# The first block's 88 projection tiles in seven products of quarters

## The chip, the cores and the metric

The kernel runs on one core of one Trainium2 chip. The metric is device time in microseconds (us); lower is better. PE is TensorE (its matmuls; PEld its weight loads), DVE VectorE, ACT ScalarE, POOL GpSimd, SP SyncE, which issues the weight transfers.

## The reference

A token sequence of 16 meta tokens and 256 real ones (width 2048, float32) goes through two blocks. The first block is one layer:

```python
xn = rmsnorm(h, norm_g[l])
(a_q, a_f, a_i, a_z, b_q, b_k, b_v, b_o, b_ig, b_fg, b_z,
 c_r, c_k, c_v, c_wd, c_ad, c_z, g_a, g_b, g_c) = split_cols(xn @ w_in[l])
y_a = hgrn2_mixer(a_q, a_f, a_i, a_z, ...)      # branch A
y_b = mlstm_mixer(b_q, b_k, b_v, b_o, b_ig, b_fg, b_z, ...)   # branch B
y_c = rwkv7_mixer(c_r, c_k, c_v, c_wd, c_ad, c_z, ...)   # branch C
merged = sigmoid(g_a) * (y_a @ w_br[l, 0]) + sigmoid(g_b) * (y_b @ w_br[l, 1]) + sigmoid(g_c) * (y_c @ w_br[l, 2])
h = h + merged @ w_out[l]
```

The mixers use silu and sigmoid of several of these projections (silu(q), sigmoid(f), sigmoid(-f), silu(z) in A; silu after a short convolution, sigmoid(o), silu(z) in B; two sigmoids of low-rank products and silu(z) in C). The second block has two layers of another kind (pooling, state space, sparse attention), each with a large input projection of its own. The product that this change touches is `xn @ w_in`, with 2048 terms for each output.

## The kernel before

Activations lie with features on the 128 partitions and the 272 tokens along the free axis (`xnT`: 16 pieces of 128 features). A tile is 128 output columns of a projection for all tokens: 16 matmuls, each with a 128x128 piece of weights held and 272 columns of `xnT` (256 where meta tokens aren't needed) streamed, summed in a PSUM bank. `ring` has four slots of 2 MB of weights, 256 columns (two tiles) each; SP fills them in order, each when the tiles of its last use are done. `section_pe` (line 289) does eight tiles from the four slots; tiles alternate between banks 0 and 1, and `section_act` (line 339) copies each into a field of `G` (`g[0]` to `g[6]`), a field being eight tiles.

The first block runs in this order on PE: eight raw tiles of branch A's q (line 307), during which the inputs are normalised; A's other 24 tiles; A's mixer with the gate tiles g_a (line 481, into `hT`) between its small products; the merge with w_br (line 515); B's 24 tiles, the input and forget gates (line 853), 8 tiles of z; B's mixer; merge; in C a low-rank tile (line 1117), 8 tiles of k, the low-rank products up (line 1127), 8 of r, the norms (line 544), 8 of v, the dot products (line 1139), 8 of z, then C's mixer. 88 tiles of these go through `section_pe`. Sigmoids are computed as exp on ACT, plus one and reciprocal on DVE (`plus_one_inverse`, lines 562 and 564), over a whole field at a time.

The second block's large projection is already done in *units* (line 367): weights and inputs are cut in quarters, and two tiles come out of seven products instead of eight. A product is eight matmuls of 128 or, with the meta tokens, 144 columns. A unit needs turned inputs (four sums and differences of quarters of `xnT`: x12, x22, x21, x11, made once) and four sums of quarters of its own weights, which DVE makes in the ring's last slot (s1, s2, s4, lines 419, 422, 432) or in place (line 428), so that three slots are left for loads. PE's seven products go to two banks, `own` and `other`; some of their intermediate states are copied out by ACT (`unit_first_act`, `unit_middle_act`, `unit_last_act`) and added by DVE (`unit_ends_dve`). The counters are `st_full` (PE), `st_act`, `st_dve` and `st_sum`; `proj_full` and `proj_free` count tiles, `work_full` and `work_free` the uses of four further banks (2 to 5, taken in turn, `wbank`), which the mixers use for small products. The order on every engine is that of the code; every wait is on a counter, and behind a waiting instruction everything on its engine waits.

## Time and profile before

| | |
|---|---|
| median of 3 runs | 3409.15 us (3408.1 to 3411.21) |
| profiled execution, its own time | 3415.68 us |
| its span | 3413.9 us |
| PE busy | 3379.4 us, 22582 instructions |
| PEld busy | 2949.7 us |
| DVE, ACT busy | 1577.5 us, 639.8 us |
| mean granted clock | 0.994 |

The profile is of one execution. Busy time of PE runs over pipelined matmuls whose ends are modelled, so stretches and starts tell more than durations. A line is that of the kernel's source; a matmul in float32 leaves two records and two weight loads. In the chain of waits each piece is a stretch in which the named line held up everything after it.

### The profile page before, as it was taken

The page shows a single profiled execution, that of the slowest core. Times are in us where ns is not written, and L with a number is a line of the kernel's source. Part 1 is how long each engine was busy: PE and PEld are TensorE (multiplying, and loading weights), DVE is VectorE, ACT ScalarE, POOL GpSimd, SP SyncE. Part 2 cuts the span into 40 slices and gives each one's busy share as a digit, 9 for nine tenths or more (in the row PEclk, how much of TensorE's full clock was granted, in tenths as well). Part 3 has the DMA queues.
Part 4 walks back from the last instruction along what each step waited for, and adds up shares of the span by engine and source line. Part 5 has one row for each costly group of instructions (what it writes and reads, how often), then busy time and mean ns, then how long its engine had stood idle before and what let it go on. Part 6 is the DMA issues. An engine that isn't in the chain of part 4 may idle for free.

```text
span 3413.9 us, 53363 instructions
## 1 busy us (share of the span) xinstructions
PE 3379.4 (99%) x22582; PEld 2949.7 (86%) x22582; DVE 1577.5 (46%) x2834; ACT 639.8 (19%) x1632; POOL 45.0 (1%) x83
## 2 busy tenths in 40 slices
PE   9999999999999999999999999999999999999999
PEld 7888888888888898888899997877779999988787
DVE  2426631324556471522455756524344566563343
ACT  1012200011011000111111216412131112352211
POOL 1000000000000000000000000000000000000000
PEclk9999999999999999999999999999999999999999
DMA  7443244433444302553444444333444544533432
GB/s 233 136 152 114 100 148 147 149 124 112 154 128 144 99 4 70 203 170 104 141 156 149 157 149 139 87 124 118 142 128 148 166 148 157 173 124 87 145 127 74
DMA packets 436422, 454.89 MB, mean 133 GB/s; under 512 B 25307, under 2 KB 412832, under 8 KB 435904
## 3 DMA queue, kind: packets, MB, share of 16 engines
q1 hardware_dynamic: 433600, 444.48, 41.1%
q0 software_dynamic: 2128, 5.19, 0.5%
q8 instruction: 175, 2.87, 0.4%
q10 hardware_dynamic: 464, 1.90, 0.1%
q14 instruction: 55, 0.45, 0.0%
HBM read 449.46 MB, written 2.10 MB: 132 GB/s over the span
## 4 chain that ended last, share of the span: by engine, by line
PE 98%; DVE 1%; ACT 0%; DVEq 0%; issue 0%; POOL 0%; ACTq 0%; POOLq 0%
PE bank L367 21%; PE bank L289 19%; PE bank L2063 10%; PE bank L481 10%; PE bank L1952 9%; PE bank L307 5%; PE bank L515 5%; PE bank L2127 3%; PE bank L1602 3%; PE bank L1162 3%; PE bank L2036 1%; PE bank L2114 1%; PE bank L2086 1%; PE bank L544 0%; PE bank L1989 0%; PE bank L687 0%
## 5 line engine op out<-in xcount | busy, mean ns | idle before, releaser
L289 PE MATMUL bank<-xnT,ring 128*128 128x272 f32 (+1 forms) x2816 | 633.2, 388 | 1.6 <-ACT wk L912 1.0
L289 PEld LDWEIGHTS bank<-xnT,ring 128*128 128x128 f32 x2816 | 535.2, 190 | 99.2 <-issue 3.3
L481 PE MATMUL bank<-xnT,ring 128*128 128x256 f32 x1536 | 343.7, 383 | 0.7 <-ACT wk L1336 0.7
L367 PE MATMUL bank<-xnT,ring 128*128 128x128 f32 (+1 forms) x2688 | 332.4, 281 | 0.0
L481 PEld LDWEIGHTS bank<-xnT,ring 128*128 128x128 f32 x1536 | 290.7, 191 | 40.9 <-ACT wk L1336 1.1
L1952 PE MATMUL bank<-xnT,ring 128*128 128x272 f32 (+2 forms) x1408 | 325.7, 390 | 0.0
L367 PEld LDWEIGHTS bank<-xnT,ring 128*128 128x128 f32 x2688 | 323.1, 191 | 1.0 <-issue 0.9
L1952 PEld LDWEIGHTS bank<-xnT,ring 128*128 128x128 f32 (+1 forms) x1408 | 260.5, 187 | 51.4 <-issue 0.7
L2063 PE MATMUL bank<-G,ring 128*128 128x272 f32 (+1 forms) x1024 | 239.4, 388 | 0.0
L367 PE MATMUL bank<-G,ring 128*128 128x128 f32 (+1 forms) x1792 | 225.3, 279 | 0.0
L2063 PEld LDWEIGHTS bank<-G,ring 128*128 128x128 f32 x1024 | 191.7, 190 | 35.7 <-issue 3.6
L367 PEld LDWEIGHTS bank<-G,ring 128*128 128x128 f32 x1792 | 215.6, 191 | 0.0
L307 PE MATMUL bank<-xnT,ring 128*128 128x272 f32 x768 | 184.8, 396 | 2.6 <-DVE xnT L319 1.9
L307 PEld LDWEIGHTS bank<-xnT,ring 128*128 128x128 f32 x768 | 145.1, 191 | 33.2 <-issue 3.1
L515 PE MATMUL bank<-G,ring 128*128 128x256 f32 x768 | 166.3, 379 | 0.0
L515 PEld LDWEIGHTS bank<-G,ring 128*128 128x128 f32 x768 | 146.0, 190 | 19.8
L564 DVE RECIPROCAL G<-G 128x272 f32<-128x272 f32 (+3 forms) x25 | 149.4, 5977 | 1.8
L339 ACT ACTIVATE G<-bank 128x272 f32<-128x272 f32 (+2 forms) x80 | 31.4, 393 | 575.9 <-PE bank L289 575.9
L562 DVE TENSOR_SCALAR G<-G 128x272 f32<-128x272 f32 (+3 forms) x25 | 16.2, 646 | 246.8 <-ACT G L909 95.2
L2063 PE MATMUL bank<-merged,ring 128*128 128x272 f32 (+1 forms) x512 | 120.5, 389 | 1.3 <-ACT G L2297 1.3
L419 DVE TENSOR_TENSOR ring<-ring 128x1024 f32<-128x1024 f32 x56 | 68.6, 1225 | 111.2 <-PE bank L367 98.9
L1602 PE MATMUL bank<-merged,ring 128*128 128x256 f32 x512 | 115.7, 385 | 1.1 <-DVEq L535 1.1
(563 smaller groups left out, 3791.0 us busy)
## 6 DMA issues: line engine op xcount, KB each, us to landing
ring<-in_w_in SPq DMA_DIRECT2D x155, 2048.0 KB, 8.3
ring<-in_w_out SPq DMA_DIRECT2D x32, 2048.0 KB, 8.3
ring<-in_w_br SPq DMA_DIRECT2D x12, 2048.0 KB, 8.9
ring<-in_w_out SPq DMA_DIRECT2D x16, 1024.0 KB, 10.7
ring<-in_w_in SPq DMA_DIRECT2D x8, 512.0 KB, 6.9
G<-in_x POOLq DMA_DIRECT2D x2, 1024.0 KB, 8.6
wk<-in_pool_w POOLq DMA_DIRECT2D x2, 1024.0 KB, 9.1
out<-G SPq DMA_DIRECT2D x8, 256.0 KB, 2.6
```

Of the source, the lines that this page charges most:

```text
L289: mm = pe.matmul(bank[j][:, first:T], ring[:, s, k, j * P:(j + 1) * P], rhs[:, k, first:T], start=(k == 0), stop=(k == KT - 1))
L307: mm = pe.matmul(bank[j][:, 0:T], ring[:, s, k, j * P:(j + 1) * P], xnT[:, k, :], start=(k == 0), stop=(k == KT - 1))
L367: mm = pe.matmul(out_, weights[:, k, :], x(k), start=(start and k == 0), stop=(k == HALF - 1), skip_group_check=True)
L419: v.tensor_tensor(s1, a21, a22, ALU.add).then_inc(S["st_sum"], 1)
L481: mm = pe.matmul(bank[j][:, META:T], ring[:, s, k, j * P:(j + 1) * P], xnT[:, k, META:T], start=(k == 0), stop=(k == KT - 1))
L515: mm = pe.matmul(bank[6 + j % 2][:, META:T], wide[:, s, k, j * P:(j + 1) * P], y[:, k, META:T], start=(k == 0), stop=(k == W8 - 1))
L564: v.reciprocal(a, a)
L1162: mm = pe.matmul(out[rows], lhsT[rows], rhs[rows], start=start, stop=stop)
L1602: pe.matmul(bank[j][:, META:T], ring[:, s, k, j * P:(j + 1) * P], merged[:, k, META:T], start=(k == 0), stop=False)
L1952: mm = pe.matmul(out_, ring[:, s, k, c:c + m], xnT[:, k, first:T], start=(k == 0), stop=(k == KT - 1))
L2063: mm = pe.matmul(bank[j][:, m0:T], ring[:, c + k // KT, k % KT, j * P:(j + 1) * P], mix[k][:, m0:T], start=(k == 0), stop=(k == SUB - 1))
L2127: mm = pe.matmul(bank[j % 2][:, m0:T], wide[:, s, k, j * P:(j + 1) * P], mix[SUB + k][:, m0:T], start=(k == 0), stop=(k == W8 - 1))
```

## The change

Branches A, B and C project their 88 tiles in 44 units. The turned inputs of the first block lie in `hT` (free until the gate tiles are written), made anew for each branch by `turn_inputs_dve`. B's gate tile moves ahead of B's units; the low-rank tile stays ahead of C's. In each unit the second product and the corner (the fourth and sixth product) go to work banks, the other five to one projection bank; ACT copies four intermediate states and then the last (five copies, four before), and DVE's adds of the second half follow each other. DVE makes the next unit's four sums one after another ahead of these adds. This form holds for the second block's 56 units too. The sigmoids come from ACT's table, in pieces of two tiles between the unit's copies; the element-wise work of the branches is spread over the units as `first_part(u)`, `second_part(u)` and `last_part(u)`; C's up products, norms and dot products stand between its units. The core of the diff:

```diff
+        def units_load(sp, src, columns, first):
+
+            for u, col in enumerate(columns):
+                s = (u + first) % (SLOTS - 1)
+                slot_load(sp, s, src[:, :, col:col + BLK])
+                last_use[s] = (proj_full, tiles["sp"].go())
+            last_use[SLOTS - 1] = (S["st_dve"], units["sp"].go(len(columns)))
...
-            own, other = bank[(t - 1) % 2], bank[t % 2]
+            own = bank[(t - 1) % 2]
...
             product(own[:, lo:MID], a11, lambda k: xnT[:, k, lo:MID], True).then_inc(S["st_full"], 1)
-            pe.wait_ge(proj_free, t + 1)
-            product(other[:, lo:MID], a12, lambda k: xnT[:, HALF + k, lo:MID], True).then_inc(S["st_full"], 1)
-            pe.wait_ge(S["st_act"], 3 * n + 1)
+            pe.wait_ge(work_free, work["pe"].go())
+            product(wbank(work["pe"].n)[:, lo:MID], a12, lambda k: xnT[:, HALF + k, lo:MID], True).then_inc(work_full, 1)
+            pe.wait_ge(S["st_act"], 4 * n + 1)
             pe.wait_ge(S["st_sum"], 4 * n + 2)
             product(own[:, META:MID], s2, lambda k: x22[:, k, :], False).then_inc(S["st_full"], 1)
-            pe.wait_ge(S["st_dve"], 3 * n + 1)
-            product(other[:, MID:T], s1, lambda k: x12[:, k, :], True).then_inc(S["st_full"], 1)
-            pe.wait_ge(S["st_act"], 3 * n + 2)
+            pe.wait_ge(work_free, work["pe"].go())
+            unit_banks.append(wbank(work["pe"].n))
+            corner = unit_banks[n][:, MID:T]
+            product(corner, s1, lambda k: x12[:, k, :], True).then_inc(S["st_full"], 1)
+            pe.wait_ge(S["st_act"], 4 * n + 2)
             pe.wait_ge(S["st_sum"], 4 * n + 3)
             product(own[:, lo:MID], a21_less, lambda k: x21[:, k, lo:MID], False).then_inc(S["st_full"], 1)
-            pe.wait_ge(S["st_act"], 3 * n + 3)
+            pe.wait_ge(S["st_act"], 4 * n + 3)
             pe.wait_ge(S["st_sum"], 4 * n + 4)
-            product(other[:, MID:T], s4, lambda k: xnT[:, HALF + k, MID:T], False).then_inc(S["st_full"], 1)
-            pe.wait_ge(S["st_dve"], 3 * n + 2)
+            product(corner, s4, lambda k: xnT[:, HALF + k, MID:T], False).then_inc(work_full, 1)
+            pe.wait_ge(S["st_act"], 4 * n + 4)
             product(own[:, lo:MID], a22, lambda k: x11[:, k, lo:MID], False).then_inc(proj_full, 1 + skip)
...
-        def unit_middle_act(act, d1, d2):
-            n, own, other = units["act"].now(), bank[tiles["act"].now() % 2], bank[(tiles["act"].now() + 1) % 2]
-            act.wait_ge(S["st_full"], 6 * n + 3)
+        def unit_second_act(act, d1):
+            n, own = units["act"].now(), bank[tiles["act"].now() % 2]
+            act.wait_ge(S["st_full"], 4 * n + 2)
             act.activation(d1[:, MID:T], own[:, META:MID], ACT.Copy).then_inc(S["st_act"], 1)
-            act.wait_ge(S["st_full"], 6 * n + 4)
-            act.activation(d2[:, MID:T], other[:, MID:T], ACT.Copy).then_inc(S["st_act"], 1)
+
+        def unit_third_act(act):
+            n = units["act"].now()
+            corner = unit_banks[n][:, MID:T]
+            work["act"].go(2)
+            act.wait_ge(S["st_full"], 4 * n + 3)
+            if n >= 2:
+                act.wait_ge(S["st_dve"], n - 1)
+            act.activation(t5_at[n % 2], corner, ACT.Copy).then_inc(S["st_act"], 1)
+
+        def unit_fourth_act(act, d2):
+            n, own = units["act"].now(), bank[tiles["act"].now() % 2]
+            act.wait_ge(S["st_full"], 4 * n + 4)
+            act.activation(d2[:, MID:T], own[:, META:MID], ACT.Copy).then_inc(S["st_act"], 1)
...
+            v.wait_ge(w_loaded[s], 16 * u)
+            if n:
+                v.wait_ge(S["st_full"], 4 * (n - 1) + 3)
+            v.tensor_tensor(s1, a21, a22, ALU.add).then_inc(S["st_sum"], 1)
+            v.drain()
+            v.tensor_tensor(s2, s1, a11, ALU.subtract).then_inc(S["st_sum"], 1)
...
+        def unit_first_dve(v, d1, lo):
+            n = units["dve"].now()
+            u = work["dve"].go()
+            corner_full[n] = work["dve"].go()
+            v.wait_ge(work_full, u)
+            v.wait_ge(S["st_act"], 4 * n + 1)
+            v.tensor_tensor(d1[:, lo:MID], d1[:, lo:MID], wbank(u)[:, lo:MID], ALU.add).then_inc(work_free, 1)
+
+        def unit_ends_dve(v, d1, d2):
+            n = units["dve"].go() - 1
+            u = corner_full[n]
+            v.wait_ge(work_full, u)
+            v.wait_ge(S["st_act"], 4 * n + 4)
+            v.tensor_tensor(d1[:, MID:T], d1[:, MID:T], wbank(u)[:, MID:T], ALU.add).then_inc(work_free, 1)
+            v.tensor_tensor(d2[:, MID:T], d2[:, MID:T], t5_at[n % 2], ALU.add).then_inc(S["st_dve"], 1)
...
+            for u in range(12):
+                dst, j = g[1 + u // 4], 2 * (u % 4)
+                unit_first_act(act, dst[:, j, :], first_from(u, 8))
+                first_part(u)
+                unit_second_act(act, dst[:, j, :])
+                unit_third_act(act)
+                second_part(u)
+                unit_fourth_act(act, dst[:, j + 1, :])
+                unit_last_act(act, dst[:, j + 1, :], first_from(u, 8))
...
+                if u == 6:
+                    act.wait_ge(S["ml_in"], c["in"].go())
+                    act.activation(ROWS[:, TMP, :], ROWS[:, TMP, :], ACT.Exp, scale=-1.0)
+                    act.drain()
+                    act.activation(ROWS[:, TMP, :], ROWS[:, TMP, :], ACT.Ln, bias=1.0).then_inc(S["ml_act"], 1)
...
+                if u == 5:
+                    wait()
+                    fn(flat(g[4]), flat(g[4]), ACT.Sigmoid)
+                if u == 6:
+                    fn(flat(g[5]), flat(g[5]), ACT.Sigmoid)
+                    wait()
+                    fn(flat(g[3]), flat(g[6]), ACT.Square)
+                if u == 8:
+                    rk["act"]["in"].go()
+                    wait()
+                    fn(flat(g[3][:, 0:4]), flat(g[3][:, 0:4]), ACT.Sqrt)
+                if u == 9:
+                    wait()
+                    fn(flat(g[3][:, 4:8]), flat(g[3][:, 4:8]), ACT.Sqrt)
+                if u == 10:
+                    fn(flat(g[4]), flat(g[4]), ACT.Exp)
...
+                if u == 7:
+                    for j in range(W8):
+                        v.tensor_tensor_scan(tmp8[:, j, :], reset, g[4][:, j, :], 0.0, ALU.mult, ALU.add)
...
+                if u == 7:
+                    v.tensor_tensor(flat(g[4]), flat(tmp8), flat(g[4]), ALU.subtract)
+                    to("rk_in")
+                    norms_out(0)
+                if u == 8:
+                    norms_out(4)
...
+                if u == 14:
+                    for j in range(W8):
+                        v.scalar_tensor_tensor(wk[:, j, :], g[0][:, j, :], vec("rwkv_r_k", 1, j), g[1][:, j, :], ALU.mult, ALU.mult)
+                    to("rk_pe")
...
+            turn_inputs_dve(v, *first_turned)
+            unit_sums12_dve(v, n0)
+            unit_sums34_dve(v, n0)
+            for u in range(16):
+                dst, j = g[(1, 0, 2, 3)[u // 4]], 2 * (u % 4)
+                unit_first_dve(v, dst[:, j, :], first_from(u, 12))
+                first_part(u)
+                if u + 1 < 16:
+                    unit_sums12_dve(v, n0 + u + 1)
+                    unit_sums34_dve(v, n0 + u + 1)
+                unit_ends_dve(v, dst[:, j, :], dst[:, j + 1, :])
+                tiles["dve"].go()
+                second_part(u)
...
-            section_pe(pe, 2, xnT)
-            section_pe(pe, 1, xnT, META)
+            pe.wait_ge(S["st_turned"], count["pe"]["st_turned"].go())
+            for u in range(12):
+                unit_pe(pe, u % 3, first_from(u, 8), *first_turned)
             hgrn_pe(pe)
             merge_pe(pe, 0, g[4])
-            section_pe(pe, 2, xnT)
-            section_pe(pe, 1, xnT, META)
             mlstm_gates_pe(pe)
-            section_pe(pe, 1, xnT, META)
+            pe.wait_ge(S["st_turned"], count["pe"]["st_turned"].go())
+            for u in range(16):
+                unit_pe(pe, (u + 1) % 3, first_from(u, 8), *first_turned)
             mlstm_pe(pe)
             merge_pe(pe, 1, g[4])
             rwkv_low_rank_pe(pe)
-            section_pe(pe, 1, xnT)
-            rwkv_up_pe(pe)
-            section_pe(pe, 1, xnT)
-            rwkv_norms_pe(pe)
-            section_pe(pe, 1, xnT)
-            rwkv_dots_pe(pe)
-            section_pe(pe, 1, xnT, META)
+            pe.wait_ge(S["st_turned"], count["pe"]["st_turned"].go())
+            for u in range(16):
+                unit_pe(pe, (u + 1) % 3, first_from(u, 12), *first_turned)
+                if 1 <= u <= 4:
+                    rwkv_up_pe(pe, 2 * u - 2)
+                if u in (7, 8):
+                    rwkv_norms_pe(pe, 4 * (u - 7))
+                if u == 14:
+                    rwkv_dots_pe(pe)
```

The instructions of PE behind the merge of branch B, where the low-rank tile of C stands first. Before (names: output bank, inputs, columns, and how often in a row):

```order
L1117 MATMUL bank0<-xnT,ring 128x272 x16
L283 UNCONDITIONAL_BRANCH
L289 MATMUL bank0<-xnT,ring 128x272 x16
L289 MATMUL bank1<-xnT,ring 128x272 x16
L289 MATMUL bank0<-xnT,ring 128x272 x16
```

The same place now, one unit (hT holds the turned inputs):

```order
L1315 MATMUL bank0<-xnT,ring 128x272 x16
L377 MATMUL bank0<-xnT,ring 128x144 x8
L377 MATMUL bank3<-xnT,ring 128x144 x8
L377 MATMUL bank0<-hT,ring 128x128 x8
L377 MATMUL bank4<-hT,ring 128x128 x8
L377 MATMUL bank0<-hT,ring 128x144 x8
L377 MATMUL bank4<-xnT,ring 128x128 x8
L377 MATMUL bank0<-hT,ring 128x144 x8
L377 MATMUL bank1<-xnT,ring 128x144 x8
```

Two tiles of 32 matmuls became seven products of eight; banks 3 and 4 are work banks, and the next unit goes on in bank 1.

DVE in branch C, where the scans (line 1425 before, 1664 now) and the eviction of the norms (1431, 1642) stand. Before:

```order
L564 RECIPROCAL G<-G 128x2176
L1422 TENSOR_SCALAR G<-G 128x2176
L1425 SCALAR_TENSOR_TENSOR tok<-fc,G 128x272 x8
L1427 TENSOR_TENSOR G<-tok,G 128x2176
L562 TENSOR_SCALAR G<-G 128x2176
L564 RECIPROCAL G<-G 128x2176
L1431 TENSOR_SCALAR G<-bank3 128x272
```

Now, unit 7 of C, from its first addition (462) to the next unit's:

```order
L462 TENSOR_TENSOR G<-G,bank5 128x144
L1664 SCALAR_TENSOR_TENSOR tok<-fc,G 128x272 x8
L442 TENSOR_TENSOR ring<-ring 128x1024
L444 TENSOR_TENSOR ring<-ring 128x1024
L450 TENSOR_TENSOR ring<-ring 128x8x128
L454 TENSOR_TENSOR ring<-ring 128x1024
L469 TENSOR_TENSOR G<-G,bank2 128x128
L470 TENSOR_TENSOR G<-G,ring 128x128
L1691 TENSOR_TENSOR G<-tok,G 128x2176
L1642 TENSOR_SCALAR G<-bank3 128x272
```

The reciprocals are gone, and the four sums of the next unit and the three additions of this one stand between the scans and the norms.

ACT in branch C, end of unit 5 to the beginning of unit 7 (405, 410, 419, 424 and 430 are the unit's five copies):

```order
L430 ACTIVATE G<-bank1 128x144
L1509 ACT_TABLE_LOAD
L1509 ACTIVATE G<-G 128x2176
L405 ACTIVATE G<-bank0 128x144
L410 ACTIVATE G<-bank0 128x128
L419 ACTIVATE ring<-bank4 128x128
L424 ACTIVATE G<-bank0 128x128
L430 ACTIVATE G<-bank0 128x144
L1509 ACTIVATE G<-G 128x2176 x2
L405 ACTIVATE G<-bank1 128x144
```

and before, the same activations behind a section's eight copies (of which the last two stand here):

```order
L339 ACTIVATE G<-bank0 128x272
L339 ACTIVATE G<-bank1 128x272
L336 REGISTER_ALU
L336 COMPARE_AND_BRANCH
L1310 ACTIVATE G<-G 128x2176
L1310 ACT_TABLE_LOAD
L1310 ACTIVATE G<-G 128x2176
```

The long activations stood behind a whole section; now each stands between two units.

## Rows read from the trace of the kernel before

**Rows 1.** The page's first part: busy us (share of the span), instructions.
```profile
PE 3379.4 (99%) x22582; PEld 2949.7 (86%) x22582; DVE 1577.5 (46%) x2834; ACT 639.8 (19%) x1632; POOL 45.0 (1%) x83
```

**Rows 2.** The chain of waits in order of time: start us, us, what.
```profile
79.45 172.59 PE bank L289 x768
...
647.44 55.49 PE bank L289 x256
...
912.05 58.90 PE bank L289 x256
...
1039.94 58.67 PE bank L289 x256
1102.38 55.47 PE bank L289 x256
...
1661.49 158.60 PE bank L367 x1344
...
1827.42 211.21 PE bank L367 x1792
...
2587.75 150.28 PE bank L367 x1344
```

**Rows 3.** Groups by line and form, line 289: busy us, mean ns, idle before.
```profile
L289 PE MATMUL bank<-xnT,ring 128*128 128x272 f32 x1792 | 411.7, 393 | 0.6 <-ACT tok L1313 0.6
...
L289 PE MATMUL bank<-xnT,ring 128*128 128x256 f32 x1024 | 221.8, 379 | 1.0 <-ACT wk L912 1.0
```

**Rows 4.** Windows: length, busy of PE PEld DVE ACT POOL, PEclk, DMA, GB/s.
```profile
1661.00:1820.00 159.00, 159.00 (x1348) 158.58 (x1346) 85.93 (x137) 26.70 (x76) 0.00 (x0) 1.00 0.51 160
...
912.00:1157.00 245.00, 244.82 (x1085) 202.84 (x1086) 134.03 (x101) 30.92 (x48) 0.00 (x0) 1.00 0.46 146
382.00:390.00 8.00, 7.72 (x34) 7.02 (x33) 0.58 (x3) 1.15 (x3) 0.00 (x0) 0.57 0.62 233
```

**Rows 5.** Timeline, second block, first and last of the turned inputs: start, us.
```profile
1622.35 1.23 DVE L2396 TENSOR_TENSOR merged<-xnT 128x1024 f32<-128x1024 f32 x1
...
1626.35 1.23 DVE L2403 TENSOR_TENSOR tok<-xnT,G 128x1024 f32<-128x1024 f32 x1
```

**Rows 6.** Timeline, end of B's merge and C's first section.
```profile
904.70 0.43 DVE L534 TENSOR_TENSOR merged<-merged,hT  x1 [0.16 <-issue]
...
912.05 3.22 PE L289 MATMUL bank<-xnT,ring 128*128 128x272 f32 x13 [0.64 <-ACT tok L1313]
```

**Rows 7.** Timeline, a unit of the second block from its fifth product on.
```profile
1861.15 2.13 PE L367 MATMUL bank<-G,ring 128*128 128x144 f32 x16
1861.35 0.28 ACT L402 ACTIVATE G<-bank 128x128 f32<-128x128 f32 x1 [1.51 <-PE bank L367]
...
1865.09 0.29 DVE L447 TENSOR_TENSOR G<-G,bank 128x128 f32<-128x128 f32 x1 [0.36 <-PE bank L367]
...
1866.61 1.23 DVE L432 TENSOR_TENSOR ring<-ring 128x1024 f32<-128x1024 f32 x1
```

**Rows 8.** Groups of DVE in branch C's projections.
```profile
L564 DVE RECIPROCAL G<-G 128x2176 f32<-128x2176 f32 x2 | 27.5, 13753 | 0.1
L1476 DVE RECIPROCAL wk<-wk 128x256 f32<-128x256 f32 x8 | 14.0, 1753 | 0.6
...
L1425 DVE TENSOR_TENSOR_SCAN tok<-fc,G 128x272 f32<-128x272 f32 x8 | 5.0, 701 | 0.1
...
L1431 DVE TENSOR_SCALAR G<-bank 128x272 f32<-128x272 f32 x8 | 3.5, 442 | 8.6 <-PE bank L544 8.5
...
L562 DVE TENSOR_SCALAR G<-G 128x2176 f32<-128x2176 f32 x2 | 2.6, 1295 | 0.3
...
L1427 DVE TENSOR_TENSOR G<-tok,G 128x2176 f32<-128x2176 f32 x1 | 2.4, 2425 | 0.1
```

**Rows 9.** Timeline of ACT: a table switch in B, a long activation in C.
```profile
703.72 1.28 ACT L917 ACT_TABLE_LOAD   x1
705.01 0.43 ACT L917 ACTIVATE wk<-wk 4x272 f32<-4x272 f32 x1
...
1036.61 2.01 ACT L1310 ACTIVATE G<-G 128x2176 f32<-128x2176 f32 x1
```

More of the change, by code:

```diff
@@ L918, in mlstm_act @@
-            act.activation(real(g[6]), real(g[3]), ACT.Exp, scale=-1.0).then_inc(S["ml_act"], 1)
+            z_sigmoid(3)
             gates_act(act, 2)
@@ L1332, in rwkv_act @@
             wait()
-            for j in range(W8):
-                act.wait_ge(proj_full, tiles["act"].go())
-                act.activation(g[3][:, j, META:T], bank[j % 2][:, META:T], ACT.Copy)
-                act.activation(wk[:, j, META:T], bank[j % 2][:, META:T], ACT.Exp, scale=-1.0).then_inc(proj_free, 1)
+            act.drain()
+            act.wait_ge(S["st_dve"], n0 + 16)
+            fn(real(wk), real(g[3]), ACT.Sigmoid)
             def turned():
@@ L1390, in to @@
                 v.nop().then_inc(S[name], 1)
-            t0 = tiles["dve"].go(34) - 34
-            def shift(src, tmp, mu):
-                v.tensor_tensor(tmp[:, :, 1:T], src[:, :, 0:T - 1], src[:, :, 1:T], ALU.subtract)
-                v.tensor_scalar(tmp[:, :, 0:1], src[:, :, 0:1], -1.0, None, ALU.mult)
-                v.drain()
-                v.tensor_tensor(tmp, tmp, across(vec("rwkv_mu", 8, mu)), ALU.mult)
-                v.drain()
-                v.tensor_tensor(flat(src), flat(src), flat(tmp), ALU.add)
+            t0, n0 = tiles["dve"].go(2) - 2, units["dve"].now()
@@ L1470, in rwkv_dve @@
             to("rk_pe")
[L1471 to L1478 removed]
+            acted(10)
+            v.tensor_tensor(real(g[3]), real(g[3]), real(wk), ALU.mult)
             to("rk_in")
@@ L2172, in layers_act @@
         def layers_act(act):
+            unit_base = units["act"].now()
             def wait(name, k=1):
@@ L2527, in pool_ends @@
                     to("b2_in")
-                n0 = UNITS * layer
+                n0 = units["dve"].now()
                 for j in range(W8 - 1):
```

630 lines of the change are left out of this document (377 added, 253 removed).

## The prediction

> **What bounds the kernel now.** I read the page first: PE is busy 99% of the span [rows 1], so only what shortens or stalls the matmul stream moves the time. Then the chain of waits in order of time: the first block's plain projections (line 289) stand in it as unbroken pieces, two of 172.59 us (the first stands in the rows), one of 55.49, three near 58.8 (58.90 to 58.67) and one of 55.47 [rows 2]. They add up to 632.6 us. Grouped by form they are 1792 records with 272 columns and 1024 with 256 [rows 3]; one matmul leaves two records, 16 matmuls make a tile, so that is 56 tiles of 272 tokens and 32 of 256, the 88 of the change. The second block already runs "units": two tiles in seven products of quarters. They stand in the same chain, also without a gap [rows 2]. Last come the stretches: in a unit stretch PEld is busy 158.58 of 159 us, the weight loads are the limit there, the granted clock is 1.00 and DVE works 85.93 us; in the third branch's projections DVE works 134.03 of 245 us, which no wait of PE shows [rows 4].
>
> **The change part by part.** *The products.* Two plain tiles become 56 matmuls of 144 or 128 columns. What such a unit takes is read from the second block: 1344 records are 12 units, 158.60 us or 13.22 each with the 16 meta tokens; 1792 records are 16 units, 211.21 us or 13.20 each; the layer that leaves the meta tokens out has 12 units in 150.28 us, 12.52 each [rows 2]. The first block gets 44 units: 8 with meta tokens and 4 without in branch A, 8 and 8 in B, 12 and 4 in C, so 28 x 13.21 + 16 x 12.52 = 369.9 + 200.3 = 570.2 us. Against 632.6 that is 62.4 us less. The pace is measured on the same instruction with the same weights in the ring and operands in SBUF, so I take it unchanged. Streaming alone would allow seven eighths of 632.6, a gain of 79.1; that is the end I keep above.
>
> *Getting started.* Each branch first needs the turned inputs (five DVE instructions that took from 1622.35 to 1626.35 + 1.23, so 5.2 us [rows 5]), and PE waits for them. In A they lie under the raw tiles, which run until 79.45 [rows 2]. In B and C, PE has one other tile in front (the input gates, the low rank). In C the merge's last DVE instruction ends at 905.13; 5.2 us later is 910.4, and PE's first projection started at 912.05 anyway, after waiting for that tile's eviction [rows 6]. The order rows show that B now has its gate tile in the same place. Cost nothing, 1.6 us of cover; without it 5.2 us a branch. The first four sums (4 x 1.23 = 4.9 us [rows 7]) trail by less than the two products that need none of them and then one product each.
>
> *Inside a unit.* 128-column products take 12.52/7 = 1.79 us, 144-column ones (13.21 - 3 x 1.79)/4 = 1.96. ACT starts 0.20 us after a product's end and copies in 0.28 (1861.15 to 1861.35 [rows 7]). Each copy has at least one product (1.79 us) to hide under; with two work banks the first product's addition and the corner no longer hold PE's two projection banks. DVE owes a unit 4 x 1.23 + 3 x 0.29 = 5.8 us [rows 7] of 13.2. So a unit stalls only where something long sits in between. I followed ACT's order, counting from the end E of a unit: its last copy is done at E + 0.48, and its next one must be done before the third product at E + 3.92.
> - C, unit 6: two activations over 2176 elements, 2.01 each [rows 9], then the copy 0.28 and some 0.1 of hand-over: E + 4.9, a stall of 1.0.
> - C, units 5 and 10: a table load of 1.28 and one such activation: E + 4.15, 0.25 each, together 0.5.
> - B, unit 6: two table loads and two short activations of 0.43 [rows 9]: E + 4.3, 0.35.
> - C, unit 7, on DVE: eight scans of 0.70 (5.6), then the next sums, the ends, a 2.43 us subtraction, and only then the eviction of the norms' first bank (0.44) [rows 8]. From the unit's start: second product done and added 4.4, scans 10.1, three sums 13.9, fourth sum and ends 15.7, subtraction 18.2, eviction 18.75. Unit 8's second product wants that bank; it could start at 14.2 + 1.9 (norms) + 1.96 = 18.05. Stall 0.8.
> Sum 2.65, say 2.7. Where the scans or reciprocals (a quarter of a field, 13.75/4 = 3.44, twice in unit 10 [rows 8]) run late, the next product's bank runs late with them: the end I keep there is 1 us in each of the last eleven C units.
>
> The Trainium skill ("ScalarE: Activation LUTs", What ACT_TABLE_LOAD costs) prices a switch of table at 1283 ns plus a drain of 1380. Here the load at 703.72 ends at 705.00 and the activation starts at 705.01 [rows 9]: the load agrees, the drain does not show. By the page the four loads named above would cost 5.5 us more, and the forecast would be 3355.
>
> *Sigmoids from the table.* The sigmoids' reciprocals (13.75 us a field [rows 8]) leave DVE. None of them holds PE in the chain, so I book nothing; what they do is make room: 134.03 - 27.5 - 2.6 (two whole fields, reciprocal and plus one) - 14.0 (eight tiles of z) + 16 x 5.8 + 5.2 = 188 us of DVE work in C's some 220 us of units [rows 4, 8]. The reciprocal of the norms stays.
>
> *Tail of C.* After the last unit DVE has an addition, two more, a clear, the three parts of a shift and the copies: seven instructions like the 2.425 us one [rows 8] and some 2.5 us of small ones, 19.5 us. PE has 64 gate matmuls in front of the first wait, half of the 128 in 55.47 us [rows 2], 27.7. Hidden by 8 us.
>
> *Second block.* Same products in the same order; two go to work banks, the four sums are issued together ahead of the ends, and ACT has one copy more, with its second part between the third and the fourth. That copy has two products, 3.75 us, to be ready. DVE was busy 54% there [rows 4]. I take nothing; 0.1 us a unit would be 5.6, and a gain is excluded because the pieces have no gap to give.
>
> The sum: -62.4 + 2.7 = -59.7 us. The profiled execution took 3415.68 and is 6.5 above the median 3409.15; it consists of the same stretches, so I subtract from the median: 3349.4.
>
> **Rivals.**
> 1. *Queues late in C and at the seams.* DVE at some 85% in C leaves little, and every part there waits for ACT and the other way round; 11 units at 1 us, and perhaps one fall of the clock, which at 382 to 390 us held 0.57 over 8 us and cost 3 to 4 [rows 4]. Against it: each late step I found has its slack. Gain 50 to 45, time 3359 to 3364.
> 2. *A larger gain.* If stalls don't come and waits of about a microsecond at starts (the 0.64 at 912.05 [rows 6]) shrink: 62.4 + 2, and a little from B's end, where DVE no longer has a reciprocal: 3343 to 3346.
> 3. *Slower: DVE paces the units.* Its place is DVE's part ahead of the next unit's sums: in the new order s1 and s2 stand behind the whole first part, and that waits for ACT, which waits for DVE's last unit. If that circle is longer than a unit, PE waits at its third product in every unit. It decides from 62.4/44 = 1.42 us a unit; at 2 us in 44 units it is +88 - 62 = 26 slower, 3435. For it: the heaviest C units have 12.7 us of DVE work in 13.2. Against it: A and B have far lighter parts (about 4 us), and s1, s2 are asked for 10 us after the fourth product lets DVE begin.
> 4. *It doesn't do what it says:* the narrow products in the first block run slower than the second's. Nothing in the rows differs; I hold it inside rival 1.
>
> **How the numbers follow.** Forecast 0.70 (3345 to 3355), rival 1 with 4 0.20, rival 2 0.06, rival 3 0.04. The range cuts off half of rival 2, the far end of 1 and all of 3: 3343 to 3366. No change means within 0.2%, 6.8 us, about what this kernel's measurement can tell. Faster by more: 0.95; within 0.01; slower 0.04.
>
> **What would show it.** Line 289 gone from the chain; three unit stretches of about 156, 206 and 209 us (C with some 14 us of small products beside); PEld near 100% and clock 1.00 in them; PE's waits in C small, the largest at units 7 and 8, named ACT's 2176-element activation and DVE's norm eviction; the second block's stretches still 158.6, 211.2 and 150.3. Wrong would be: unit stretches over 13.4 us a unit, a repeating wait at the third product, a clock below 1.00 in them, or second-block pieces longer than before.

## The result, and the profile after

The changed kernel takes 3345.16 us (median of 4 runs, 3341.99 to 3349.47) against 3408.62 (4 runs, 3408.04 to 3411.21) for the kernel before on the same chip: ratio 0.9816, 95% interval 0.9804 to 0.9828, 63 us less. The forecast was 3349.4 with 3343 to 3366. All that follows reads the execution of the changed kernel that was profiled, 3348.12 us with a span of 3346.3.

The page's first part, against [rows 1]:

```profile
PE 3311.6 (99%) x24694; PEld 2977.4 (89%) x24694; DVE 1672.5 (50%) x3172; ACT 705.1 (21%) x1883; POOL 45.1 (1%) x83
```

PE has 68 us less work in 2112 more records; DVE has 95 us more: the weight sums (44 units of 4.9 us) came, and the 149 us of reciprocals and their additions went (that figure is from e3 below). PE is still the bound.

The chain of waits in order of time (start us, us, what), against [rows 2]:

```profile
80.14 155.62 PE bank L377 x1344
...
458.62 92.65 PE bank L377 x784
...
555.33 109.60 PE bank L377 x976
...
874.04 26.64 PE bank L377 x224
945.35 26.85 PE bank L377 x224
...
1003.80 77.36 PE bank L377 x672
...
1595.57 158.60 PE bank L377 x1344
1761.50 211.21 PE bank L377 x1792
2520.78 150.27 PE bank L377 x1344
2677.96 208.44 PE bank L377 x1792
```

Line 289 is gone. Branch A's 24 plain tiles took 172.59 us and now take 155.62. B's stretch is one piece but for one break at 555: 206.3 us. C is broken up by the other tiles between its units (the dot products, norms and low rank), 223.96 us from 874.04 to 1098.00. Counted with the gate tile and the low-rank tile, from the first projection matmul of the branch to the last, B went from 236.5 (466.44 to 702.93) to 214.7 (450.20 to 664.92) and C from 254.5 to 231.9. That is 17.0, 21.8 and 22.6 us, 61.3 in all. The four stretches of the second block are what they were, to 0.01 us (the fourth, not in [rows 2], was 208.44 too).

The three unit stretches by windows (us, then busy time and instructions of PE, PEld, DVE, ACT, POOL, granted clock, DMA share, GB/s), against [rows 4]:

```profile
80.10:235.80 155.70, 155.70 (x1346) 155.69 (x1345) 82.61 (x125) 33.81 (x98) 0.00 (x0) 1.00 0.48 149
458.60:664.90 206.30, 206.13 (x1793) 205.94 (x1794) 107.74 (x164) 39.41 (x115) 0.00 (x0) 1.00 0.49 154
874.00:1098.00 224.00, 222.56 (x1857) 216.22 (x1857) 155.47 (x176) 38.14 (x91) 0.00 (x0) 1.00 0.45 142
```

PEld is busy all the time in A and B, as in the second block (in C 216 of 224 us, with the small tiles between the units), and the granted clock is 1.00, the 2.4 GHz level. DVE does 6.9, 6.7 and 9.7 us of work a unit.

PE's waits of the changed kernel from 60 to 1160 us (engine line waited for: us in total, times, longest):

```profile
PE bank L377 <- ACT wk L1020: 1.0, 1, 1.0
PE bank L377 <- ACT tok L1512: 0.6, 1, 0.6
PE bank L377 <- DVE G L1642: 0.6, 1, 0.6
...
PE bank L377 <- ACT G L405: 0.5, 1, 0.5
```

The first two are the starts of B and C behind the eviction of the tile ahead. The other two are in C, and the timeline shows both (start us, us, engine line; in brackets the idle time before):

```profile
972.40 3.92 ACT L1509 ACTIVATE G<-G 128x2176 f32<-128x2176 f32 x2
976.22 0.28 ACT L405 ACTIVATE G<-bank 128x144 f32<-128x144 f32 x1
...
976.55 5.80 PE L377 MATMUL bank<-hT,ring 128*128 128x128 f32 x48 [0.46 <-ACT G L405]
...
977.00 5.03 DVE L1664 TENSOR_TENSOR_SCAN tok<-fc,G 128x272 f32<-128x272 f32 x8
...
987.41 2.43 DVE L1691 TENSOR_TENSOR G<-tok,G 128x2176 f32<-128x2176 f32 x1
...
989.97 1.49 DVE L1642 TENSOR_SCALAR G<-bank 128x272 f32<-128x272 f32 x4
990.46 2.23 PE L377 MATMUL bank<-xnT,ring 128*128 128x144 f32 x16 [0.57 <-DVE G L1642]
```

The two activations of 2176 elements stand between two units' copies; the unit's first copy comes at 976.22 and PE's third product waits for it. Behind the scans, the sums and the subtraction the norms' first bank is read out at 989.97, and unit 8's second product waits for it.

One more thing moves the total: stretches in which the clock is granted at less than 1.00. I take windows of 4 us over the span and add (1 - clock) x 4. Before this gives 20.5 us, after 13.6. The rest of a span is then 3393.4 before and 3332.7 after, 60.7 apart. The pieces give 61.3, and A's units begin 0.7 us later than A's tiles did (80.14 against 79.45), so the two agree. None of these falls lies in a unit stretch.

### The profile page after: what moved, and what is told of

Same layout as the page of the kernel before. It is cut to its first block, busy times and chain, and to the rows that moved or that the text cites. A ratio compares the mean times of both kernels' runs of the same rounds, so it can differ in the third digit from the quotient of the medians.

```text
span 3346.3 us, 58431 instructions
## 1 busy us (share of the span) xinstructions
PE 3311.6 (99%) x24694; PEld 2977.4 (89%) x24694; DVE 1672.5 (50%) x3172; ACT 705.1 (21%) x1883; POOL 45.1 (1%) x83
## 4 chain that ended last, share of the span: by engine, by line
PE 98%; DVE 1%; ACT 1%; DVEq 0%; issue 0%; ACTq 0%; POOL 0%; POOLq 0%
PE bank L377 38%; PE bank L2333 10%; PE bank L524 10%; PE bank L2222 10%; PE bank L315 5%; PE bank L558 5%; PE bank L2397 3%; PE bank L1872 3%; PE bank L1360 3%; PE bank L2306 1%; PE bank L2384 1%; PE bank L2356 1%; PE bank L2259 0%; PE bank L766 0%; PE bank L2362 0%; PE bank L1003 0%
## 5 line engine op out<-in xcount | busy, mean ns | idle before, releaser
L377 PE MATMUL bank<-xnT,ring 128*128 128x128 f32 (+1 forms) x4800 | 593.2, 280 | 2.2 <-ACT wk L1020 1.0
L377 PEld LDWEIGHTS bank<-xnT,ring 128*128 128x128 f32 x4800 | 575.7, 191 | 6.4 <-issue 5.2
L377 PE MATMUL bank<-hT,ring 128*128 128x128 f32 (+1 forms) x2816 | 339.0, 279 | 0.6 <-ACT G L405 0.5
L377 PEld LDWEIGHTS bank<-hT,ring 128*128 128x128 f32 x2816 | 330.2, 191 | 1.4 <-ACT G L405 1.4
L524 PEld LDWEIGHTS bank<-xnT,ring 128*128 128x128 f32 x1536 | 289.6, 190 | 40.3 <-ACT G L430 0.6
L442 DVE TENSOR_TENSOR ring<-ring 128x1024 f32<-128x1024 f32 x100 | 122.5, 1225 | 236.6 <-PE bank L377 193.5
L315 PEld LDWEIGHTS bank<-xnT,ring 128*128 128x128 f32 x768 | 145.0, 191 | 33.4 <-issue 3.1
L462 DVE TENSOR_TENSOR G<-G,bank 128x144 f32<-128x144 f32 (+1 forms) x100 | 29.9, 299 | 273.4 <-PE bank L377 265.8
L454 DVE TENSOR_TENSOR ring<-ring 128x1024 f32<-128x1024 f32 x100 | 122.5, 1225 | 9.6 <-PE bank L377 0.5
L444 DVE TENSOR_TENSOR ring<-ring 128x1024 f32<-128x1024 f32 x100 | 122.5, 1225 | 9.2
L450 DVE TENSOR_TENSOR ring<-ring 128x1024 f32<-128x1024 f32 x100 | 121.9, 1219 | 0.0
```

What stands on the lines that cost most here:

```text
L315: mm = pe.matmul(bank[j][:, 0:T], ring[:, s, k, j * P:(j + 1) * P], xnT[:, k, :], start=(k == 0), stop=(k == KT - 1))
L377: mm = pe.matmul(out_, weights[:, k, :], x(k), start=(start and k == 0), stop=(k == HALF - 1), skip_group_check=True)
L442: v.tensor_tensor(s1, a21, a22, ALU.add).then_inc(S["st_sum"], 1)
L444: v.tensor_tensor(s2, s1, a11, ALU.subtract).then_inc(S["st_sum"], 1)
L450: v.tensor_tensor(a21, a11, a21, ALU.subtract).then_inc(S["st_sum"], 1)
L454: v.tensor_tensor(s4, a12, s2, ALU.subtract).then_inc(S["st_sum"], 1)
```

## The experiments

Every run below has its median against the kernel before on the same chip. "Lost" is the sum over clock falls just described, and "rest" the profiled span less it.

| | median us | ratio, 95% | span | lost | rest |
|---|---|---|---|---|---|
| before | 3408.62 | 1 | 3413.9 | 20.5 | 3393.4 |
| changed kernel | 3345.16 | 0.9816 (0.9804 to 0.9828) | 3346.3 | 13.6 | 3332.7 |
| e1 the same again | 3342.60 | 0.9810 (0.9796 to 0.9823) | 3340.1 | 8.5 | 3331.6 |
| e2 stalls mended | 3346.86 | 0.9818 (0.9804 to 0.9832) | 3345.1 | 15.4 | 3329.7 |
| e3 sigmoids only | 3410.22 | 1.0007 (0.9997 to 1.0016) | 3407.5 | 13.6 | 3393.9 |
| e4 A in plain tiles | 3364.73 | 0.9870 (0.9855 to 0.9885) | 3366.2 | 15.3 | 3350.9 |
| e5 inputs turned twice | 3358.60, two runs | 0.9857 (0.9828 to 0.9886) | 3356.1 | 17.1 | 3339.0 |
| e6 three more sums a unit | 3394.81 | 0.9951 (0.9927 to 0.9974) | 3392.6 | 30.8 | 3361.8 |
| e7 seven more sums | 3612.57, one run | | 3610.8 | 119.5 | 3491.3 |
| e8 extra matmuls at the start | 3503.86, one run | | 3502.1 | 27.3 | 3474.8 |
| e9 additions ahead of the next unit | 3358.45 | 0.9858 (0.9841 to 0.9874) | 3355.0 | 12.0 | 3343.0 |
| e10 three more sums, A and B only | 3352.71, two runs | 0.9836 (0.9814 to 0.9858) | 3355.3 | 20.4 | 3334.9 |

**e1, the changed kernel again, in five rounds.** No edit.

> The changed kernel once more, five rounds against the kernel before. Theory: the units give 61.4 us (16.97 in branch A, 21.8 in B, 22.6 in C, by the profiled pieces), and what the profiled execution gained beyond that, some 6 us, is falls of the granted clock that one execution has and another has not (20.5 us lost in the profile of before, 13.6 in that of after). So the median gain over rounds is 61 to 64 us, and single times scatter by multiples of about 3.4 us; a profile has A, B and C pieces of the same length within 0.3 us whatever its time. Rival: the extra 6 us belong to the change (DVE freed from reciprocals): the gain is 66 to 68 in every round.

3342.60 us, which is 65.7 under the 3408.29 of before: above the 61 to 64 of the theory and just under the 66 to 68 of the rival, so the totals leave open which of the two holds. The fastest runs of the two kernels, 3404.38 and 3341.92, lie 62.5 apart. Each piece of the chain has its length again (155.62, 92.65, 109.60, 26.64 and so on). Two profiled executions of one kernel lie 6.2 us apart in span, about 5.1 of it in clock falls and 1.3 in the start before A. So of one execution of this kernel, anything under some 7 us is read from the pieces, not from the total.

**e2, the three stalls taken away.** One long activation of C and half of B's pair go one unit later, and the norms' eviction goes ahead of the subtraction.

```diff
                 if u == 6:
-                    fn(flat(g[5]), flat(g[5]), ACT.Sigmoid)
                     wait()
                     fn(flat(g[3]), flat(g[6]), ACT.Square)
+                if u == 7:
+                    fn(flat(g[5]), flat(g[5]), ACT.Sigmoid)
...
                 if u == 7:
+                    norms_out(0)
                     v.tensor_tensor(flat(g[4]), flat(tmp8), flat(g[4]), ALU.subtract)
                     to("rk_in")
-                    norms_out(0)
```

> The changed kernel with its three named stalls taken apart: of C's unit 6 the sigmoid over 2176 elements goes behind unit 7; the norms' banks are evicted ahead of the subtraction in unit 7; in B the exponential stays behind unit 6 and the logarithm goes behind unit 7. Theory (long activations and an eviction stand between a unit's copies): the stalls of 0.6 (third product of unit 7), 0.7 (second product of unit 8) and 0.3 us (B) vanish, 1.6 us faster than the changed kernel. Rival (the stall is table switches or DVE load in general): they move to the next unit, no gain.

B's units are one piece of 205.89 us instead of 206.30, C's stretch is 222.60 instead of 223.96; of PE's waits at line 377 only the two starts (1.0 and 0.6 us) are left in the list. So the three places were named rightly, and they are worth 0.4 (B) + 1.36 (C) = 1.8 us, where 1.6 was expected. The total (3346.86, its interval over that of e1) can't tell this from nothing: the profiled execution lost 6.9 us more to clock falls than that of e1.

**e3, the sigmoids alone, in the kernel before.** Exponential, plus one and reciprocal become the table's sigmoid in the three branches; all tiles stay plain.

```diff
-            act.activation(flat(g[5]), flat(f), ACT.Exp, scale=-1.0).then_inc(S["hg_exp"], 1)
+            act.activation(flat(g[5]), flat(f), ACT.Sigmoid).then_inc(S["hg_exp"], 1)
...
-            plus_one_inverse(v, flat(g[5]))
```

> The kernel before, plain tiles, with only the sigmoids of the first block taken from the scalar table: no add and reciprocal on DVE, no units. Theory: DVE's reciprocals stood beside PE's work and held nothing, so the time is that of before within 2 us (DVE busy falls by some 110 us all the same). Rival: the sigmoids are part of the gain, 3 to 7 us faster than before.

Ratio 1.0007 (0.9997 to 1.0016) with 149 us less of DVE work (1428.5 us busy on its page, 1577.5 in [rows 1]; I had expected 110).

The plain pieces are as long as before (172.59, 172.59, 55.49, 58.91, 58.87, 58.67, 55.47). The reciprocals held up nothing there.

**e4, branch A back in plain tiles** and with its reciprocals (which e3 showed to cost nothing), the rest as changed.

```diff
-            section_load(sp, w_in[0], A_COL, 1)
-            units_load(sp, w1, [A_COL + 1024 + BLK * u for u in range(12)], 0)
+            section_load(sp, w_in[0], A_COL, 4)
...
-            for u in range(12):
-                unit_pe(pe, u % 3, first_from(u, 8), *first_turned)
+            section_pe(pe, 2, xnT)
+            section_pe(pe, 1, xnT, META)
```

> The changed kernel with branch A as before (24 plain tiles, sigmoids by reciprocals), units in B and C. Theory: each branch gives its own share with no interplay, A is worth 172.59 - 155.62 = 17.0 us, so 17 us slower than the changed kernel and 44 to 46 faster than before. Rival: part of A's gain is given back later (its mixer starts sooner and waits for gates), then less than 14 us slower.

```profile
79.70 172.59 PE bank L297 x768
```

A's piece is back at 172.59 us, B's units start at 475.16 instead of 458.62, and B's and C's pieces are those of the changed kernel. The rest of the span is 18.2 us above the changed kernel's, of which 17.0 is A's piece. By medians it is 19.6 us slower than the changed kernel and 43.6 faster than before, just outside the 17 and the 44 to 46 that I expected. Some 2.3 us more than in the changed kernel, beside the clock falls, lie in C's mixer (between the end of C's units and 1256 us); no run shows why. A's gain isn't given back in B's and C's units, then, and B and C have theirs without A's; that B and C are independent of each other was not tried.

**e5, the inputs turned twice in B and C.** It asks how much cover the turning has.

```diff
-            turn_inputs_dve(v, *first_turned)
+            turn_inputs_dve(v, *first_turned, again=True)
```

> The changed kernel with the turned inputs of branches B and C made twice in a row before they are released (5.3 us more of DVE each time). Theory (they are hidden by one tile and its eviction): in the changed kernel DVE is done at 456.1 in B and PE starts its units at 458.62, cover 2.5 us; in C the cover is about 1.6. So PE starts 2.8 us later in B and 3.7 in C, 6 to 7 us in all (read from the pieces' starts: 458.62 - 450.20 = 8.4 becomes 11.2, 874.04 - 866.07 = 8.0 becomes 11.7). Rival (PE's start hangs on the eviction or on loads): no shift, or the whole 10.6.

```profile
PE bank L377 <- DVEq L489: 8.3, 2, 4.5
```

The second turning takes 5.3 us more; PE waits 3.87 us at B's start and 4.5 at C's instead of 1.0 and 0.6, 6.7 us more, as expected. So the cover was 2.4 us in B and 1.4 in C. The rest of the span is 6.3 us above the changed kernel's. The median is 13 above: each of the two waits brought a fall of the clock, which no start in the changed kernel has. B's start in windows, the wait ending at 461.34:

```profile
460.00:464.00 4.00, 2.66 (x12) 2.67 (x13) 3.68 (x4) 0.00 (x0) 0.00 (x0) 0.69 1.09 365
464.00:468.00 4.00, 4.00 (x31) 4.00 (x31) 2.66 (x3) 0.29 (x1) 0.00 (x0) 0.88 0.28 87
```

1.7 us are lost there and 3.4 at C's start.

**e6 and e7, three and seven more weight sums ahead of each unit's first,** in the 44 units of the first block (the edit is that of e6; e7 has 7 for 3). They put the rival that forecast a slower kernel to the test: DVE pacing the units.

```diff
+            for _ in range(3 if n < 44 else 0):
+                v.tensor_tensor(s1, a21, a22, ALU.add)
+                v.drain()
```

> The changed kernel, first block only: DVE makes the first sum of each unit's weights four times instead of once, 3 x 1.3 = 3.9 us more of DVE in front of each unit's third product. Theory (DVE has slack in each unit; it works 6.9 us of 13 in A, 6.7 in B and 9.7 of 14 in C): A and B keep 155.6 and 206.3 us, C loses 2 to 8 us at its full units 7 to 12. Rival (the units are paced by DVE's sums, or nearly): 44 x 3.9 = up to 170 us more.

> As before with eight times the first sum, 7 x 1.3 = 9.1 us more of DVE a unit. Theory: now DVE paces every unit at its own work, 16.0 us in A, 15.8 in B, 18.8 in C: A 155.6 to about 190, B 206 to 252, C 224 to 300, in all some 150 us slower, with PE waiting for the second sum at the third product. That is the point at which the slower rival of the prediction would have decided. Rival: PE waits from the first added sum on, 44 x 9.1 = 400 us.

e6 came out worse than expected: 3394.81, some 50 us over the changed kernel. Its stretches:

```profile
80.10:240.00 159.90, 157.19 (x1349) 156.77 (x1348) 126.21 (x163) 35.62 (x100) 0.00 (x0) 1.00 0.47 146
458.60:669.00 210.40, 209.15 (x1806) 207.73 (x1805) 169.33 (x215) 41.47 (x120) 0.00 (x0) 1.00 0.48 151
876.00:1146.00 270.00, 240.01 (x1870) 229.90 (x1870) 214.95 (x229) 40.22 (x93) 0.00 (x0) 0.94 0.38 120
```

A and B carry 10.6 us of DVE work a unit with no wait of a microsecond or more that the changed kernel lacks but one, at A's start: their units end 2.3 and 2.6 us later than in the changed kernel. The other 42.6 us are in C, whose last unit ended at 1142.85 and not at 1097.64. Clock falls are 15.4 of them (the clock there is 0.94), and PE's waits the other 27. The list names what for:

```profile
PE bank L1328 <- DVE G L472: 9.8, 4, 2.4
PE bank L377 <- ACT G L405: 9.6, 2, 9.1
PE bank L590 <- DVE G L472: 8.1, 2, 5.9
```

My expectation looked at DVE's work alone, 9.7 + 3.7 = 13.4 us a unit in the mean and 16.4 in the units that I had at 12.7. That fits a part only. The 9.1 us are such a place: there DVE is busy for 16.27 of the 17 us from 1072 to 1089, and ACT waits 12.0 us for it before it copies. But the 9.8 us are four waits of 2.4 in units 1 to 4, which are not full. One of these units (window as above; then start us, us, engine line):

```profile
908.20:928.90 20.70, 18.26 (x121) 16.91 (x121) 10.94 (x15) 1.42 (x5) 0.00 (x0) 0.83 0.33 103
```

```profile
916.08 0.30 DVE L465 TENSOR_TENSOR G<-G,bank 128x144 f32<-128x144 f32 x1 [5.93 <-PE bank L377]
...
919.72 3.83 DVE L443 TENSOR_TENSOR ring<-ring 128x1024 f32<-128x1024 f32 x3 [3.34 <-PE bank L377]
...
928.87 1.27 PE L1328 MATMUL bank<-tok 64*128 64x272 f32 x2 [2.44 <-DVE G L472]
```

DVE works 10.94 us of 20.7 here and itself waits 5.93 and 3.34 us for PE. The unit is long because the two take turns: the last of the four low-rank products needs a work bank, which comes free with DVE's closing addition (line 472), and that addition stands behind the unit's sums, the added ones included, which can't begin before PE's fourth product. The norms' products (line 590) wait for the same addition: 5.9 us behind unit 7, where DVE is full (21.49 us of the 22.5 from 994.7 on), and 2.2 behind unit 8, where it isn't (12.30 of 18.8). So some 12 of the 27 us come from the order of work, and the rest from a full engine.

e7, one run, is 267 us over the changed kernel (264.5 by the spans) where 150 were expected. Its timeline in A shows the circle (start us, us):

```profile
202.29 9.03 DVE L443 TENSOR_TENSOR ring<-ring 128x1024 f32<-128x1024 f32 x7 [0.89 <-PE bank L377]
...
214.08 7.40 PE L377 MATMUL bank<-hT,ring 128*128 128x128 f32 x48 [2.27 <-DVE ring L447]
...
219.62 9.03 DVE L443 TENSOR_TENSOR ring<-ring 128x1024 f32<-128x1024 f32 x7 [0.89 <-PE bank L377]
```

A unit takes 17.33 us, DVE is idle for 1.1 of them, and PE waits at its third product for s2 (line 447) in all 28 units of A and B, just as rival 3 had it. In C it does so nine times, and waits 30.9 us at the low-rank products, 18.7 at the norms and 12.4 for an ACT copy, as in e6. The rest of the span is 158.6 us over the changed kernel's: that is the 150. The other 106 are clock falls: 119.5 us lost against 13.6, one in nearly every unit.

**e10, the three sums in A and B only.**

> As in the run with three more sums of 1.23 us ahead of each unit's first sum, but in branches A and B only (28 units of the first block); C is as in the changed kernel. It tells whether that run's 50 us were DVE work as such or the units of C alone. Theory: DVE has 6.9 and 6.7 us of work a unit in A and B, 10.6 with the extra sums, below the 13.2 of a unit, so nothing inside the branches; 2 to 3 us at the start of each, where the first sums stand before the third product; 4 to 6 us over the changed kernel, 3347 to 3350 by its median, with a clock fall or two after the two waits at most. Rival (any DVE work ahead of the sums is paid): 28 x 3.7 = 104 us, or half of it.

A's units end 2.3 us later than in the changed kernel, B's 2.6, C's 2.3: C has its old length, and the rest of the span is 2.2 us above. A began 0.6 us earlier in this execution, so the stretches themselves are 2.9 us longer in A (2.7 of it one wait for s2 at the start) and 0.4 in B. That is less than my 4 to 6, since B's start, unlike A's, cost next to nothing. The median, 3352.71 of two runs (3348.32 and 3357.10), is above my range; the profiled one of them lost 20.4 us to clock falls, 6.8 of them from 1212 on, where e1 lost 1.7. The rival is out: 28 units with 3.7 us more DVE work each cost some 3 us, not 104.

**e9, each unit waits for DVE's closing additions of the one before.** It takes away the overlap that the work banks allow, a product that starts while the last unit's corner is still unread; the banks themselves stay.

```diff
             pe.wait_ge(proj_free, t)
+            if 0 < n < 44:
+                pe.wait_ge(S["st_dve"], n)
```

> In the first block every unit but a branch's first waits, before its first product, until DVE has done the two closing additions of the unit before; the second block is unchanged. It takes away what the work banks give (a product that starts while the last unit's corner is still unread) and nothing else. In the trace of the changed kernel these additions end at about the moment at which the next unit's first matmul issues (106.33 against 106.37 us), later in C where DVE is behind. Theory (the banks buy only a hand-over): 0.2 to 0.3 us in each of 41 units and a few us at C's unit 7, 10 to 13 us over the changed kernel, 3353 to 3356, nearly all of it in the unit pieces, which would break up into one per unit. Rival (without the banks the two engines wait for one another in every unit): 1 us or more a unit, 3385 and over.

3358.45, some 2 us above the range that I gave; the rest of the span is 10.3 us up. But it is not 0.2 to 0.3 a unit: the units with meta tokens hardly notice (A's first piece is unbroken for 960 records), and each of those without takes about 13.0 us instead of 12.52:

```profile
579.19 1.95 PE L377 MATMUL bank<-hT,ring 128*128 128x128 f32 x16
580.99 0.28 DVE L472 TENSOR_TENSOR G<-G,ring 128x128 f32<-128x128 f32 x1
...
581.43 3.81 PE L377 MATMUL bank<-xnT,ring 128*128 128x128 f32 x32 [0.29 <-DVE G L472]
...
592.22 1.95 PE L377 MATMUL bank<-hT,ring 128*128 128x128 f32 x16
```

The stretches are longer by 3.0 us in A, 4.9 in B and 2.2 in C, which have 4, 8 and 4 such units. The sum that I expected was right, its distribution wrong. The chain shows where it comes from: 7.40 us of PE's first four products, then 5.63 us until DVE has made the next unit's sums and the closing additions (588.83 to 594.46 in B). Three 128-column products, at 1.79 us each by the prediction's working, are done before that; with 144 columns in two of them they take 5.7 and hide it.

**e8, PE's pace by width.** 64 matmuls of each width from 272 down to 32 columns, one after the other at the start of the program, into a bank that nobody uses.

```diff
+                for w in (272, 256, 144, 128, 112, 96, 64, 32):
+                    for _ in range(64):
+                        pe.matmul(bank[4][:, 0:w], hT[:, 0, 0:P], hT[:, 0, 0:w], start=True, stop=True)
```

> The changed kernel with 8 x 64 extra matmuls at the start, on a tile of ones, of 272, 256, 144, 128, 112, 96, 64 and 32 columns, whose results nothing reads. It measures the pace of one float32 matmul with its two weight loads by width. Theory (weight loads limit narrow ones): 272 and 256 take 460 and 432 ns as the plain tiles did, 144 takes 245, 128 takes 224 and everything below stays near 215 to 224. Rival (columns alone set the pace): 128 at 213, 64 at 107.

Windows of 272, 256, 144, 128, 64 and 32 columns, in this order (those of 112 and 96 read as that of 128 does; a matmul leaves two records):

```profile
10.00:36.00 26.00, 26.00 (x115) 21.57 (x114) 0.00 (x0) 6.07 (x9) 1.78 (x3) 1.00 1.08 356
40.00:64.00 24.00, 24.00 (x113) 21.11 (x112) 0.00 (x0) 0.00 (x0) 0.00 (x0) 1.00 0.00 1
68.00:79.00 11.00, 11.00 (x92) 11.00 (x91) 0.00 (x0) 0.00 (x0) 0.00 (x0) 1.00 0.01 1
82.00:94.00 12.00, 12.00 (x110) 12.00 (x109) 0.00 (x0) 0.00 (x0) 0.00 (x0) 1.00 0.01 1
...
124.00:136.00 12.00, 12.00 (x110) 12.00 (x109) 0.00 (x0) 0.00 (x0) 0.00 (x0) 1.00 0.01 1
142.00:162.00 20.00, 20.00 (x96) 20.00 (x95) 0.00 (x0) 0.00 (x0) 0.00 (x0) 0.50 0.00 1
```

That is some 456, 429, 242 and 220 ns a matmul for the first four, and 220 for 112, 96 and 64 columns too: 110 records in 12 us each time. The rival, 107 ns at 64 columns, is out. From 128 columns down the width no longer counts. That it is the weight load which sets this floor is the likeliest reading, as PEld is busy for all of it, but no proof: PEld reads busy throughout at 144 columns too, where a matmul takes longer. The floor is where the 79 us that a count of columns promised shrank to 62: two tiles' 32 matmuls of 272 columns are 14.7 us and 56 of 144 or 128 columns 13.2, a tenth less, where seven eighths would be 12.9.

## Why the prediction was right, point by point

- **The products.** Forecast -62.4 us. A came to 155.62 where 8 x 13.21 + 4 x 12.52 is 155.8; B to 205.9 without its stall (e2) for 205.8; the pace of the second block carried over unchanged, and e4 gives A's share back alone (17 us in its piece). B's and C's shares were not taken back one by one. e8 says why the gain stops at a tenth.
- **Getting started.** Forecast nothing, with 1.6 us of cover. The turned inputs were ready before the eviction that PE waits for anyway; e5 overran the cover in B and C and paid 6.7 us of wait; by it the cover in C is 1.4 us (1.6 forecast) and in B 2.4.
- **Stalls inside a unit.** Forecast 1.0, 0.8, 0.35 and twice 0.25, in all 2.7 us; measured 0.46, 0.57 and some 0.3 to 0.4 (B), the last two about nothing, in all 1.3 to 1.8 (e2). Three of the five places showed, B's at its forecast size and the two in C smaller. The term was too large by about a microsecond, in part because records that follow each other on one engine overlap a little: the pair of long activations starts before the copy ahead of it ends, takes 3.92 us and not 4.02, and the next copy starts at 976.22, 0.1 before they end; and the eight scans take 5.03 us where I counted 5.6. (The working of the norms' stall, 18.75 less 18.05, gives 0.7; I booked 0.8.)
- **The table loads.** The sum by the trace held. The Trainium skill ("ScalarE: Activation LUTs", What ACT_TABLE_LOAD costs) would have a drain with each, by an estimate from its figure 5.5 us in the four places. In the changed kernel the load at 1002.32, one more than those four, takes 1.28 us and the next activation starts at 1003.61, so the trace disagrees again. None of the four loads shows a drain either (in B they stand at 551.61 and 553.38, their activations at 552.90 and 554.67).

```profile
1002.32 1.28 ACT L1509 ACT_TABLE_LOAD   x1
...
1003.61 1.11 ACT L1509 ACTIVATE G<-G 128x1088 f32<-128x1088 f32 x1
```

- **Sigmoids.** Booked at nothing for the path; e3 confirms it at 1.0007. That they make room which C needs is not shown: putting them back into the unit kernel wasn't tried. e6 shows only that 3.7 us more a unit ahead of the sums, 59 us in all where the sigmoids freed 44, costs C 43, clock falls included. My sum of DVE work in C, 188 us, was close as a sum: DVE works 181 us from 866 to 1125 us. But 7 of them lie ahead of the units and 18 behind the last, covered by the gates as forecast, so that the units themselves hold 155.5.
- **Tail of C and second block.** No wait over 0.4 us at C's end; the second block's pieces kept their length.
- **The rivals.** The forecast lay 4 us above the median and 7 above that of e1. By the pieces the gain is 61.3, not 59.7: that is mostly the stalls. The other 2 to 4 us of the totals are luck as far as the forecast goes, which had nothing for them. They could be fewer clock falls (20.5 us lost before, 13.6 and 8.5 in two executions after). Whether the changed kernel has fewer of them as a rule isn't shown: e3, with the plain tiles, lost 13.6 too. Rival 1 (queues late in C) didn't come; e6 shows that 3.7 us more a unit brings it, nearly half of it at the seams with the small products. Rival 3 is the mechanism that e7 produced, from a load 8.6 us a unit higher. Its price was set too low there: a wait in each unit brings a fall of the clock with it, and I had priced the wait alone.

## What to carry to other kernels

Before tiles are cut smaller to save multiplications, measure what a matmul costs by its width: here a float32 product of 128 columns costs the same 220 ns as one of 64, so a further halving would add products without making any of them cheaper. Budget the helper engine by its work, unit by unit, and then by its order: 10.6 us in 13.2 cost nothing inside the units of A and B, and the same load cost 2.4 us a unit where a bank that PE wants next comes free only behind the helper's sums. And price a wait of PE of some 4 us as the wait and a clock fall on top: it was so for both waits of e5 (1.7 and 3.4 us lost), and for a wait of 3.98 us in the second block, beside which every profiled execution has a fall that loses 3.4 us.

## What the runs showed of the hardware

The floor of 110 ns a record in e8 was new to me; plain tiles of 272 columns hide it (PEld 21.57 us busy of 26). It is near what the Trainium skill ("TensorE: Matmul & The Clock Gate", LDWEIGHTS (loading the stationary operand)) states: a load takes its columns over 1.2 in ns, by which I estimate 107 for 128. The trace agrees within 3 ns, with two loads a float32 matmul.

The granted clock fell to 0.50, the 1.2 GHz level, in e8 while PE hadn't been idle since 8.5 us: it fell at 140 us, after 14 us of 64 columns and the first few products of 32, and a matmul of 32 columns then took some 420 ns. The fall at 364 us of the changed kernel is alike. It comes at 366.4, inside a run of 32 small products of 16 columns (line 759) and before the gap of 0.28 us behind them, so the gap is not its cause:

```profile
363.17 3.98 PE L759 MATMUL bank<-G 128*128 128x16 f32 x32
...
367.43 1.22 PE L780 MATMUL bank<-merged,tok 128*128 128x256 f32 x2 [0.28 <-DVE merged L871]
```

```profile
366.00:366.40 0.40, 0.40 (x6) 0.40 (x5) 0.15 (x1) 0.00 (x0) 0.00 (x0) 0.89 0.94 364
366.40:366.80 0.40, 0.40 (x4) 0.40 (x3) 0.19 (x1) 0.00 (x0) 0.00 (x0) 0.50 1.05 410
```

So PE busy in every window is no proof of a full clock; the granted clock has to be read beside it. The falls in the profiled executions come in about 1.7 us of loss or multiples of it, and the same place loses 1.7 in one execution and 3.4 in the next (364 us in e1 and after). Of the 6.2 us between the two profiled executions of the changed kernel this is most; the other executions weren't profiled.
